# Keeping the spread conditions of the first stage for the later modulation blocks, and dealing these out anew

## The reference, cut to what matters

```
mod = silu(cond) @ w_ada + b_ada                  # 6 x 1024 values for each of 2 conditions
shift1, scale1, gate1, shift2, scale2, gate2 = mod
h = rmsnorm(x) * (1 + scale1) + shift1
q, k, v, m_q, m_k, m_v, m_o, m_i, m_f, cv_b, cv_c, cv_x, gates = split(h @ w_in)
merged = g0 * (attention(q, k, v) @ w_br_na) + g1 * (mlstm(...) @ w_br_m) + g2 * (conv(...) @ w_br_cv)
x = x + gate1 * rmsnorm(merged @ w_out)
h2 = rmsnorm(x) * (1 + scale2) + shift2
x = x + gate2 * rmsnorm((silu(h2 @ w_gate) * (h2 @ w_up)) @ w_down)
```

## Time and profile before

| | |
|---|---|
| runs | 1117.64, 1117.72, 1118.89 us, median 1117.72 |
| span of the profiled execution | 1116.2 us; its own time isn't listed apart, the median lies 1.5 above the span |
| TensorE | busy 1095.2 us (98%), 7088 matmuls |
| VectorE | busy 812.2 us (73%) |
| ScalarE | busy 530.6 us (48%) |
| POOL | busy 89.8 us (8%) |
| DMA | 141.78 MB moved, mean 127 GB/s |

### The profile page before, as it was taken

The page is one execution under the profiler, slowest core; times in us unless marked ns, Lnnn a source line. Parts: engine busy times, 40 slices in busy tenths (PEclk is TensorE's granted clock), DMA queues, the critical chain, the costliest instruction groups (busy, mean ns, idle before and its releaser), DMA issues.

```text
span 1116.2 us, 18505 instructions
## 1 busy us (share of the span) xinstructions
PE 1095.2 (98%) x7088; PEld 1029.1 (92%) x7088; DVE 812.2 (73%) x1446; ACT 530.6 (48%) x1004; POOL 89.8 (8%) x149
## 2 busy tenths in 40 slices
PE   6999999999999999999999999999999999999997
PEld 4799998789999999999999988999999999988886
DVE  5748987869878788886778647999987777633434
ACT  5534453535444336655653248555555555433431
POOL 2052322000000021010000012000000000000002
PEclk9999999999999999999999999999999999999999
DMA  9675662453721203444266345134322332424112
GB/s 367 236 238 162 187 191 75 135 168 99 68 62 40 69 27 100 159 143 152 77 208 218 99 151 170 59 131 145 120 77 77 119 108 77 132 70 175 57 38 95
DMA packets 42918, 141.78 MB, mean 127 GB/s; under 512 B 9392, under 2 KB 10960, under 8 KB 41168
## 3 DMA queue, kind: packets, MB, share of 16 engines
q1 hardware_dynamic: 38752, 131.64, 37.0%
q0 software_dynamic: 4080, 8.97, 2.5%
HBM read 127.93 MB, written 12.60 MB: 126 GB/s over the span
## 4 chain that ended last, share of the span: by engine, by line
PE 67%; DVE 0%; ACT 0%; issue 0%; POOLq 0%; POOL 0%; ACTq 0%
PE ps L2414 22%; PE ps L2415 22%; PE ps L2416 22%; PE ps L2800 0%; PE ps L2773 0%; PE ps L2606 0%; PE ps L2604 0%; ACT h L1674 0%; DVE bo_lo L1790 0%; DVE x L2393 0%; ACT bo_hi L1322 0%; DVE h_lo L2384 0%; ACT yb_junk L1344 0%; DVE x L2397 0%; ACT tmp_sb L1618 0%
## 5 line engine op out<-in xcount | busy, mean ns | idle before, releaser
L2416 PE MATMUL ps<-h_hi,w_lo 128*128 128x320 f32 x880 | 271.9, 309 | 0.0
L2415 PE MATMUL ps<-h_lo,w_hi 128*128 128x320 f32 x688 | 212.6, 309 | 0.0
L2414 PE MATMUL ps<-h_hi,w_hi 128*128 128x320 f32 x624 | 195.5, 313 | 0.1
L2416 PEld LDWEIGHTS ps<-h_hi,w_lo 128*128 128x128 f32 x880 | 165.2, 188 | 0.0
L2414 PE MATMUL ps<-w_hi,h_hi 128*128 128x512 f32 x418 | 164.8, 394 | 0.0
L2416 PE MATMUL ps<-w_hi,h_lo 128*128 128x512 f32 x418 | 162.8, 390 | 0.0
L2415 PE MATMUL ps<-w_lo,h_hi 128*128 128x512 f32 x418 | 162.8, 389 | 0.0
L2415 PEld LDWEIGHTS ps<-h_lo,w_hi 128*128 128x128 f32 x688 | 129.2, 188 | 0.1
L1699 DVE TENSOR_TENSOR w_lo<-raw,w_hi 128x1024 fp32r<-128x1024 f32 x85 | 102.6, 1221 | 32.3 <-ACT w_hi L1239 31.3
L1239 ACT ACTIVATE w_hi<-raw 128x1024 fp32r<-128x1024 f32 x85 | 88.3, 1054 | 69.3 <-PE ps L2416 62.9
L2414 PE MATMUL ps<-h_hi,w_lo 128*128 128x320 f32 x384 | 119.1, 310 | 0.0
(11 more groups left out here) (314 smaller groups left out, 2126.4 us busy)
## 6 DMA issues: line engine op xcount, KB each, us to landing
raw<-in_w_blocks SPq DMA_DIRECT2D x182, 512.0 KB, 3.9
ada<-in_w_first SPq DMA_DIRECT2D x8, 1024.0 KB, 20.0
gdram<-stage SPq DMA_DIRECT2D x8, 640.0 KB, 6.9
gt<-gdram SPq DMA_DIRECT2D x8, 640.0 KB, 4.8
xline<-x SPq DMA_DIRECT2D x5, 512.0 KB, 5.1
x<-xline SPq DMA_DIRECT2D x5, 512.0 KB, 7.7
xt<-in_x_sample SPq DMA_DIRECT2D x4, 512.0 KB, 5.7
condr<-in_cond_rows POOLq DMA_DIRECT2D x2, 1024.0 KB, 7.9
```

Of the source, the lines that this page charges most:

```text
L2414: nc.tensor.matmul(dst, wh, xh, start=first, stop=False, skip_group_check=resumed)
L2415: nc.tensor.matmul(dst, wh, xl, start=False, stop=False, skip_group_check=resumed)
L2416: return nc.tensor.matmul(dst, wl, xh, start=False, stop=last, skip_group_check=resumed)
```

## The change

`condr_a` and `prod_a` now lie at the start of their region, where `condr0` and the first scratch row lay, and queries and keys behind them. So the first stage's spread conditions are `condr_a` itself, loaded and put through Silu once; the second load, the second Silu and the wait for it are gone. The table of modulation blocks is new: two behind each part of q0 and k0, fewer later, four behind the last parts of mk and mv.

```diff
 def adas_behind(kind, which, p):
     if kind in ("mk", "mv"):
-        return 5 if p == 3 else 0
-    if (kind, which) == ("mq", 1):
-        return 2 if p == 0 else 0
-    if kind in ("q", "k", "mq") and (kind, which) != ("q", 0):
-        return 1 + p
+        return 4 if p == 3 else 0
+    if which == 0 and kind in ("q", "k") or (kind, which, p) == ("q", 1, 0):
+        return 2
+    if kind in ("q", "k", "mq"):
+        return 0 if (kind, which, p) == ("mq", 1, 1) else 1
     return 0
...
-        (naq, nak, vctx, vg, condr_a, prod_a, kct, bm, braw, sx, pt), _e = chain(
+        (condr_a, prod_a, naq, nak, vctx, vg, kct, bm, braw, sx, pt), _e = chain(
...
-        condr0 = at("condr0", [P, 2, D], R1)
-        prod0s = [at(f"dot{c}", [P, D], R1 + 8192 + 4096 * c) for c in range(2)]
+        prod0s = [prod_a, at("dot1", [P, D], R1 + 12288)]
...
-            pool.dma_start(condr0[:, :, :], src).then_inc(condr_in, 16)
+            pool.dma_start(condr_a[:, :, :], src).then_inc(condr_in, 16)
...
-                    src = bass.AP(a["cond_rows"].tensor, 0, [[0, P], [D, 2], [1, D]])
-                    pool.dma_start(condr_a[:, :, :], src).then_inc(condr_in, 16)
...
-                    if UNITS[n][:2] == ("k", 0) and part == 0:
-                        act.wait_ge(condr_in, 32)
-                        nc.scalar.activation(condr_a[:, :, :], condr_a[:, :, :], ACT.Silu).then_inc(condr_rd, 1)
...
                 if adas_done(b) == 1:
-                    dve.wait_ge(condr_rd, 2)
+                    dve.wait_ge(condr_rd, 1)
```

More of the change, by code:

```diff
@@ L686, in program @@
         mask_na = cst[:, 544:640].rearrange("p (y k) -> p y k", y=3)
-        (naq, nak, vctx, vg, condr_a, prod_a, kct, bm, braw, sx, pt), _e = chain(
-            R1, ("naq", [P, 4, T], F32), ("nak", [P, 4, T], F32), ("vctx", [P, 2, 512], F32),
-            ("vg", [P, 2, 2, 2, P], F32), ("condr_a", [P, 2, D], F32), ("prod_a", [P, D], F32), ("kct", [P, 4, CTX], F32), ("bm", [P, 3, 2, NKEY], F32),
+        (condr_a, prod_a, naq, nak, vctx, vg, kct, bm, braw, sx, pt), _e = chain(
+            R1, ("condr_a", [P, 2, D], F32), ("prod_a", [P, D], F32), ("naq", [P, 4, T], F32), ("nak", [P, 4, T], F32),
+            ("vctx", [P, 2, 512], F32), ("vg", [P, 2, 2, 2, P], F32), ("kct", [P, 4, CTX], F32), ("bm", [P, 3, 2, NKEY], F32),
             ("braw", [P, 2, 512], F32), ("sx", [P, 2, 2, NKEY], F32), ("pt", [P, 2, 2, NKEY], F32))
@@ L1489, in _ @@
                     n, part = BLOCKS[step[1]]
-                    if UNITS[n][:2] == ("k", 0) and part == 0:
+                    if UNITS[n][:2] == ("br", (1, 0)):
                         act.wait_ge(condr_in, 32)
-                        nc.scalar.activation(condr_a[:, :, :], condr_a[:, :, :], ACT.Silu).then_inc(condr_rd, 1)
-                    if UNITS[n][:2] == ("br", (1, 0)):
-                        act.wait_ge(condr_in, 48)
                         nc.scalar.activation(condr[:, :, :], condr[:, :, :], ACT.Silu).then_inc(condr_rd, 1)
@@ L1526, in _ @@
                     act.wait_ge(condr_in, 16)
-                    nc.scalar.activation(condr0[:, :, :], condr0[:, :, :], ACT.Silu).then_inc(condr_rd, 1)
+                    nc.scalar.activation(condr_a[:, :, :], condr_a[:, :, :], ACT.Silu).then_inc(condr_rd, 1)
                 elif step[0] == "h" and step[1] > 3:
@@ L2050, in _ @@
                     if BLOCKS[step[1]][0] == UNIT_OF[("br", (1, 1))]:
-                        dve.wait_ge(condr_rd, 3)
+                        dve.wait_ge(condr_rd, 2)
                 elif step[0] == "att_split":
@@ L2093, in _ @@
                         ins = nc.vector.scalar_tensor_tensor(prod0s[c][:, :], ada0[:, k, m * D:(m + 1) * D], 1.0,
-                                                             condr0[:, c, :], ALU.mult, ALU.mult,
+                                                             condr_a[:, c, :], ALU.mult, ALU.mult,
                                                              accum_out=mod[:, m, k, c:c + 1])
```

## The result

The changed kernel takes 1123.28 us (median of 4 runs, 1121.06 to 1124.54) where the kernel before takes 1117.68 (median of 4, 1117.45 to 1118.89); the ratio is 1.0042, with a 95% interval of 1.003 to 1.0055. It is slower, by 3 to 6 us. The forecast was 1118.7 with a range of 1117.0 to 1120.9; the time lies above it.

What follows compares the result with a forecast made beforehand. TensorE, busy 1095.2 of 1116.2 us, was taken as the bound, so only its stands count. Terms 1.5 + 0.3 + 0.2 - 1.0 = +1.0 give a 1117.2 span; with the median 1.5 above, 1118.7 us, range 1117.0 to 1120.9.

Steps and rivals of the forecast that it cites:

- The kept spread: First stage: dropping the second 1 MB load, the Silu and VectorE's 14.7 us wait is by itself worth 0.
- VectorE's course up to block 7: q0's second block: VectorE's `w_lo` ends at 65.05 against TensorE's need at 65.80, in time by 0.7 us.
- POOL beside VectorE: Six bias builds from 64.55 delay VectorE by 0.25 to 0.5 us each; TensorE loses 0 to 1.0, taken as +0.3.
- blocks 10 and 13: k0's two weight blocks: wanted by TensorE at 72.84 and 79.88, forecast in time with 1.8 and 0.7 us in hand.
- Queues: SP's bias load goes out later, POOL's chain starts up to 1 us later, first reader VectorE at 91.5: costs 0.
- Block 19: q1's second block, now split behind the first scores' adds, reductions and exponentials: TensorE stands 1.5 us at 95.67, +1.5.
- End of mk: End of the mLSTM key projection: block 40's split precedes the last adds, the 1.3 us stand stays and grows by +0.2.
- Gate statistics: Turn of the statistics: the last split moves ahead of VectorE's scans, so the 1.0 us stand goes, -1.0.
- The 0 for the mLSTM units behind it: mLSTM and everything later keep their order, so they cost 0.
- The late load: Rival: block 18's load, issued near 81.5, takes 8.4 us, making block 19 late by 2.6; 1120.2 us; chance 0.12.
- The full lock: Rival: each of six POOL biases holds VectorE 0.70 us, making blocks 10 and 13 late; +2.7, 1120.4 us; chance 0.14.
- The sign that I had named for being wrong: Forecast wrong if q1's second block is ready by 95.7, or if TensorE waits for a DMA before 92.

Runs made afterwards that it cites:

- q1 earlier: Changed kernel with one modulation block moved from behind q1's first block to behind mq1's second; 1119.96 us, ratio 1.0015.
- the two kernels without block 16's stand: Changed kernel with the first six bias builds replaced by memsets (1120.22 us), and with POOL's value copies held until block 16's weights landed (1120.27 us).
- mk's splits later: Changed kernel with value copies ahead of bias builds, one modulation block moved from q1 to mq1, mk's four splits one part later; 1117.97 us, ratio 0.9992.
- second profile: Changed kernel run again without edit beside the kernel before; 1121.87 us beside 1118.35, ratio 1.0033.

## Why the prediction was wrong, step by step

- *The kept spread, 0.* Right (ratio 1.0007 alone).
- *VectorE's course up to block 7.* Right: `w_lo` was forecast to end at 65.05 and ended at 65.03, less the 1.67 us of this profile's start.
- *POOL beside VectorE, +0.3.* This is the step that failed. I priced each build by what it takes from VectorE, 0.25 to 0.5 us, and compared the sum with VectorE's slack. That price was near (0.47 on average, 2.8 us for six), and blocks 10 and 13 were in time, as forecast. What I left out is the other side: a dot product holds the build too. Together they took turns, about one build for each instruction of VectorE: VectorE's starts are 1.68 apart (72.27 and 73.95) where alone they are 1.14 to 1.15, and POOL's six builds took 9.43 us. The rows that I used showed it already: beside the stretched pair of scalings the two builds at 157.51 took 1.76 us, where two of the first six took 1.40. The Trainium skill (SBUF — State Buffer, section "SBUF: two separate sides") says that the two engines exclude each other for the whole instruction. By it, as an estimate from the rows, VectorE's starts would lie 1.15 + 0.70 = 1.85 apart; at 1.68 the trace agrees in kind and stays somewhat below. The exclusion cuts both ways, and I applied it to VectorE alone.
- *Queues, 0.* Wrong, in part for the same reason. I said POOL's chain would be up to 1 us late and looked at its first reader, VectorE at 91.5. The copies were 7.6 us late (78.85 less 1.67, against 69.62): 5.2 by the stretched builds (9.43 less 4.21) and 2.3 because the builds began late, the load of the raw biases having taken longer than I allowed. Whether the 2.3 alone would do harm no run shows. What mattered was not who reads the biases but what is queued behind them: 1 MB of value copies, which then fell on block 16's load. In place of 0.3 and 0 the runs show +2.5 and +2.8.
- *Block 19, +1.5.* 1.60 was measured, for the reason given, and moving the block removes it (q1 earlier: 0.00). The agreement has luck in it: in the two kernels without block 16's stand it is 2.2 and 2.5, since the adds start 0.65 and 1.05 us later than I had them (92.97 and 93.62, less 0.82 and 1.07 of the start, against 91.5). With block 16's stand TensorE was late as well, which hid part of this.
- *End of mk, +0.2.* Right: +0.24, and block 40's split is the cause (mk's splits later: stand 0.2).
- *Gate statistics, -1.0.* Right: the stand is gone, -1.0. The 0 for the mLSTM units behind it was +0.6 in the first profile and -0.08 in the second.
- *The rivals.* The late load was the right event with the wrong load and cause: I had 8.4 us for block 18 as a chance event, it was 8.2 for block 16 by POOL's copies. The argument against it, that a competing 1 MB is gone from there, overlooked that another 1 MB came in. The full lock was right in kind, but its price per build was too high (0.70, measured 0.47) and its places, blocks 10 and 13, had no stand. The two were treated as separate cases; one is the other's cause. The sign that I had named for being wrong, a TensorE wait on a DMA before 92, is what happened: block 16's stand hangs on its load.
- *The sum with this term right.* 1.6 + 2.5 + 0.2 - 1.0 = 3.3, that is 1121.0: just below the four runs of the first measurement (from 1121.06) and among the five of the second (1120.07 to 1123.55). The rest of the first, median 1123.28, is not accounted for beyond its profile's late start and the mLSTM units.

## What to carry to other kernels

When work is moved into the idle time of one engine beside another with which it takes turns, price both engines, and follow the slowed one's queue to its end: the cost may come out at a transfer that starts several microseconds later on a full DMA stretch. An idle stretch in which another engine works is not free time. And a forecast's rivals should be tried for whether one causes the other before each is given its own chance.

## What the runs showed of the hardware that was not expected

- A VectorE dot product over 128x1024 and a POOL add over 128x256, both from SBUF, take turns when both are back to back: 1.75 instead of 1.22 us and about 1.6 instead of 0.70. Memsets on POOL beside the same dot products cost nothing (1.22 to 1.23).
- A 512 KB weight load issued behind 1 MB of POOL's copies and its 512 KB bias load took 8.2 us and hardly moved at first: from 80.6 to 83 us SP's queue had 2 packets to POOL's 188. With the copies held back and the bias load still there it had 106 to 116, and the load took 4.3 us.
- Behind a stand of TensorE the granted clock fell to one half for 3.4 us in two of the profiled executions (after waits of 2.43 and of 0.98 us), at 1.6 and 1.5 us; behind waits as long (2.17 in the changed kernel, 2.54 in its second profile) it stayed at 1.00. So a stand can cost more than its length, and not every time.
- The first loads move everything behind them, by 1.67 us in one profile of the changed kernel and 0.26 in the other, and by -0.15 to 1.95 over all kernels here; this is why medians are compared here by ratio and profiles from a mark on.
